# Gates computed inside the prompt pipeline, and one running order of 36 weight tiles over two stages

## The reference, cut to what matters

```python
proj = jnp.einsum('btd,dc->btc', h, w_in)
(a_u, a_g, b_q, b_k, b_v, b_i, b_f, b_o, b_g,
 c_q, c_k, c_v, c_g, d_q, d_g) = jnp.split(proj, SPLIT_POINTS, axis=-1)
...
i_pre = (b_i + gate_bias[0]).astype(jnp.float32)
logf = jax.nn.log_sigmoid((b_f + gate_bias[1]).astype(jnp.float32))
hb, C, n, m = mlstm(b_q.reshape(B, T, ML_HEADS, ML_DK), b_k.reshape(B, T, ML_HEADS, ML_DK),
                    b_v.reshape(B, T, ML_HEADS, ML_DV), i_pre, logf, C0, n0, m0)
...
yc = stick_breaking(c_q.reshape(B, T, SB_HEADS, SB_DIM), k_all, v_all, pos0, sb_bias)
yc = yc.reshape(B, T, GROUP_WIDTH) * jax.nn.silu(c_g)
yd = mem_attention(d_q.reshape(B, T, MEM_HEADS, MEM_DIM), mem_k, mem_v).reshape(B, T, GROUP_WIDTH)
yd = yd * jax.nn.silu(d_g)
```

## Time and profile before

| | us |
|---|---|
| median of 3 runs | 1418.17 |
| lowest, highest | 1414.91, 1420.5 |
| the profiled execution's own time | 1413.02 |
| its span | 1411.3 |
| PE busy | 1247.4 (88%) |
| DVE busy | 807.8 (57%) |
| ACT busy | 471.1 (33%) |
| POOL busy | 373.2 (26%) |

### The profile page before, as it was taken

How to read it: one execution, slowest core, us unless ns; L and a number is a source line. 1 busy time by engine, 2 the same in 40 slices (tenths; PEclk the granted TensorE clock), 3 DMA queues, 4 the chain that set the end, 5 groups by cost and what they waited for, 6 DMA issues and landing times. The chain is left out here.

```text
span 1411.3 us, 22662 instructions
## 1 busy us (share of the span) xinstructions
PE 1247.4 (88%) x7624; PEld 1050.7 (74%) x7624; DVE 807.8 (57%) x1098; ACT 471.1 (33%) x872; POOL 373.2 (26%) x245
## 2 busy tenths in 40 slices
PE   6986999998989637999898994999999999799998
PEld 5884767777766337899898984887878777467886
DVE  5658898998854514868486692344424443524121
ACT  6523556465365412132221314322213131412111
POOL 2475444353400005646556461000000000000000
PEclk9997999999999968999898997999989999899999
DMA  8765576674742408545556531855656544544320
GB/s 292 215 205 192 185 254 192 201 245 145 248 149 87 146 18 253 175 150 181 166 177 206 168 102 56 257 165 154 193 163 205 164 150 149 194 141 146 103 60 30
DMA packets 200917, 235.80 MB, mean 167 GB/s; under 512 B 13555, under 2 KB 122418, under 8 KB 200794
## 3 DMA queue, kind: packets, MB, share of 16 engines
q1 hardware_dynamic: 195682, 218.30, 49.8%
q0 software_dynamic: 5120, 16.06, 3.2%
HBM read 213.78 MB, written 20.63 MB: 166 GB/s over the span
## 5 line engine op out<-in xcount | busy, mean ns | idle before, releaser
L2091 POOL TENSOR_TENSOR bp_keys<-bp_keys,bp_q 128x1024 f32<-128x1024 f32 x64 | 167.0, 2637 | 130.9 <-DMA bp_keys<-cache_sb_k 130.7
L2091 POOL TENSOR_TENSOR cp_keys<-cp_keys,cp_q 128x1024 f32<-128x1024 f32 x64 | 161.8, 2549 | 137.9 <-DMA cp_keys<-cache_sb_k 137.7
L150 PE MATMUL bank<-xh,b_w_hi 128*128 128x344 f32 x480 | 162.3, 338 | 7.0 <-DVE b_w_lo L133 7.0
L150 PE MATMUL bank<-xl,b_w_hi 128*128 128x344 f32 x480 | 157.2, 328 | 0.0
L150 PE MATMUL bank<-xh,b_w_lo 128*128 128x344 f32 x480 | 157.0, 327 | 0.0
L150 PE MATMUL bank<-xh,d_w_hi 128*128 128x344 f32 x384 | 130.6, 340 | 26.9 <-ACT d_w_hi L128 19.3
L246 PE MATMUL bank<-xh,c_w_hi 128*128 128x344 f32 x384 | 129.7, 338 | 0.9 <-DVE c_w_lo L225 0.9
L246 PE MATMUL bank<-xl,c_w_hi 128*128 128x344 f32 x384 | 125.9, 328 | 0.0
L246 PE MATMUL bank<-xh,c_w_lo 128*128 128x344 f32 x384 | 125.8, 328 | 0.0
L150 PE MATMUL bank<-xl,d_w_hi 128*128 128x344 f32 x384 | 125.6, 327 | 0.0
L150 PE MATMUL bank<-xh,d_w_lo 128*128 128x344 f32 x384 | 125.6, 327 | 0.0
(11 more groups left out here) (386 smaller groups left out, 2495.3 us busy)
## 6 DMA issues: line engine op xcount, KB each, us to landing
cp_keys<-cache_sb_k SPq DMA_DIRECT2D x128, 256.0 KB, 2.8
cp_values<-cache_sb_v SPq DMA_DIRECT2D x128, 256.0 KB, 3.0
bp_keys<-cache_sb_k SPq DMA_DIRECT2D x128, 256.0 KB, 3.2
dp_values<-cache_sb_v SPq DMA_DIRECT2D x128, 256.0 KB, 2.8
b_w_raw<-w_in SPq DMA_DIRECT2D x20, 512.0 KB, 5.5
d_w_raw<-w_in SPq DMA_DIRECT2D x16, 512.0 KB
o_raw<-w_out SPq DMA_DIRECT2D x8, 1024.0 KB, 5.4
c_w_raw<-w_in SPq DMA_DIRECT2D x14, 512.0 KB, 5.2
```

What stands on the lines that cost most here:

```text
L150: last = self.nc.tensor.matmul(self.bank(j, c)[:, 0:self.width], w[:, s, k, :], x[:, k, c * self.width:(c + 1) * self.width], start=(k == ...
L2091: self.nc.gpsimd.tensor_tensor(self.keys[:, s], self.keys[:, s], q, ALU.mult).then_inc(self.scaled.sem, 1)
```

## The change

**One flow of tiles.** `Projection` is replaced by `Flow`, made once. It counts 36 tiles in one running order: 20 of the mLSTM and 16 of the memory stage. Tile j lies in slot j % 2; raw tiles lie in the first half of a ring (the buffer in which the prompt's page keys lie until iteration 2), and high and low parts in buffers that the prompt's tiles use too. Its semaphores are never cleared between these stages.

```diff
+    def load(self, sp, j, columns):
+        if j >= 2:
+            sp.wait_ge(self.hi_ready, j - 1)
+            sp.wait_ge(self.lo_ready, j - 1)
+        sp.sem_inc(self.loading, 1)
+        sp.dma_start(self.raw[:, j % 2], columns).then_inc(self.landed[j % 2], 16)
+    def split_hi(self, act, j):
+        act.wait_ge(self.landed[j % 2], 16 * (j // 2 + 1))
+        if j >= 2:
+            act.wait_ge(self.projected, 3 * (j - 1))
+        self.nc.scalar.activation(self.hi[:, j % 2], self.raw[:, j % 2], ACT.Copy).then_inc(self.hi_ready, 1)
```

```diff
+        self.tiles += [("IF", 0), ("G", GT - 1)]
         self.tile_of = {t: j for j, t in enumerate(self.tiles)}
...
-        for n, t in enumerate((("K", i + 1), ("G", i), ("Q", i + 1), ("V", i + 1))):
+        for n, t in enumerate((("K", i + 1) if i + 1 < GT else ("IF", 0), ("G", i), ("Q", i + 1), ("V", i + 1))):
...
                 load_values(i + 1, 0, 4)
+                if i + 2 == GT:
+                    sp.wait_ge(keys.z_ready.sem, keys.z_ready.at(GT - 1, NP))
+                    flow.load(sp, 0, k.w_in[:, :, B_K:B_K + P])
+                    flow.load(sp, 1, k.w_in[:, :, B_V:B_V + P])
...
+                if i == GT - 1:
+                    if u in (SPLIT, SPLIT + 1):
+                        act.wait_ge(stream.projected, stream.made(len(tiles)))
+                        flow.split_hi(act, u - SPLIT)
+                    if u == SOFTEN:
+                        load_tables(nc, act, LN_EXP)
+                        gates.soften(act)
+                        load_tables(nc, act, SIGMOID)
+            load_tables(nc, act, LN_EXP)
+            gates.exponents(act)
...
+                if i == GT - 1:
+                    if u == 3:
+                        stream.wait_taken(dve, tile_of["IF", 0], 2)
+                        gates.add_bias(dve)
+                    if u == SUMS:
+                        gates.sums(dve)
+                    if u == CARRY:
+                        gates.carry(dve)
+                    if u == TOPS:
+                        gates.tops(dve)
+                    if u in (SPLIT, SPLIT + 1):
+                        flow.split_lo(dve, u - SPLIT)
...
                         store(i, 0)
                     if i + 1 < GT:
                         keys.multiply_keys(pool, i + 1, r)
+            pool.wait_ge(keys.z_ready.sem, keys.z_ready.at(GT - 1, NP))
+            gates.load(pool)
+            gates.to_rows(pool)
+            gates.turn_ends(pool)
+            store(GT - 1, 0)
+            gates.turn_carried(pool)
+            gates.store(pool)
             store(GT - 1, 1)
-            pool.wait_ge(mix_out[0], 16 * GT)
-            pool.wait_ge(mix_out[1], 16 * GT)
+            gates.finish(pool)
```

The steps of `Gates` that stand in units 3 to 11:

```diff
+    def to_rows(self, pool):
+        k, G = self.k, self.G
+        pool.wait_ge(self.biased, 1)
+        pool.sem_inc(self.sending, 1)
+        pool.dma_start(k.gates_dram, self.source[0:G, 0:T]).then_inc(self.to_dram, 16)
+        pool.dma_start(k.new_gates_dram, self.source[0:G, T:NT]).then_inc(self.to_dram, 16)
+        pool.wait_ge(self.to_dram, 32)
+        pool.dma_start(self.i_row, k.gates_dram[0:MLH, :].rearrange("h (c t) -> (h c) t", t=P)).then_inc(self.from_dram, 16)
+        pool.dma_start(self.f_row, k.gates_dram[MLH:G, :].rearrange("h (c t) -> (h c) t", t=P)).then_inc(self.from_dram, 16)
+        pool.dma_start(self.new, k.new_gates_dram.rearrange("g b -> b g"),
+                       allow_slow_non_contiguous=True).then_inc(self.from_dram, 16)
+    def soften(self, act):
+        act.wait_ge(self.from_dram, 48)
+        for dst, src, s in ((self.soft, self.f_row, self.row_act), (self.new_soft, self.new[:, MLH:self.G], self.new_act)):
+            self.nc.scalar.activation(dst, src, ACT.Abs).then_inc(s, 1)
+            act.wait_ge(s, 1)
+            self.nc.scalar.activation(dst, dst, ACT.Exp, scale=-1.0).then_inc(s, 1)
+            act.wait_ge(s, 2)
+            self.nc.scalar.activation(dst, dst, ACT.Ln, bias=1.0).then_inc(s, 1)
...
+        dve.wait_ge(self.row_act, 3)
...
+    def turn_ends(self, pool):
+        k = self.k
+        pool.wait_ge(self.row_step, 5)
+        pool.sem_inc(self.sending, 1)
+        pool.dma_start(k.ends_dram.rearrange("k r -> r k"), self.ends, allow_slow_non_contiguous=True).then_inc(self.ends_out, 16)
+        pool.wait_ge(self.ends_out, 16)
+        pool.dma_start(self.end_rows, k.ends_dram.rearrange("(o k) r -> o (k r)", o=1)).then_inc(self.ends_in, 16)
...
+    def carry(self, dve):
+        nc, s, R = self.nc, self.row_step, self.R
+        nc.vector.memset(self.m_row, 0.0).then_inc(s, 1)
+        nc.vector.tensor_tensor_scan(self.soft, self.k.a_rows, self.k.a_rows, FAR * 1e4, ALU.max, ALU.max).then_inc(s, 1)
+        dve.wait_ge(s, 7)
+        dve.wait_ge(self.ends_in, 16)
...
+    def turn_carried(self, pool):
+        k = self.k
+        pool.wait_ge(self.row_step, 12)
+        pool.sem_inc(self.sending, 1)
+        pool.dma_start(k.m_prev_dram.rearrange("(o r) -> o r", o=1), self.m_prev_row).then_inc(self.m_out, 16)
+        pool.wait_ge(self.m_out, 16)
+        pool.dma_start(self.m_prev, k.m_prev_dram.rearrange("(r o) -> r o", o=1),
+                       allow_slow_non_contiguous=True).then_inc(self.m_in, 16)
...
+    def tops(self, dve):
+        nc, s = self.nc, self.row_step
+        dve.wait_ge(self.m_in, 16)
+        nc.vector.tensor_scalar(self.top, self.soft, self.m_prev, None, ALU.max).then_inc(s, 1)
+        dve.wait_ge(s, 13)
```

```diff
+            for half in range(2):
+                sp.wait_ge(k.mix_out[half], 16 * GT)
+            sp.wait_ge(k.mix_done, 16 * MLH)
...
-                    act.wait_ge(mix_out.sem, mix_out.at(i, 0))
+                    act.wait_ge(mix_out, 16 * i)
+                else:
+                    for half in range(2):
+                        act.wait_ge(k.mix_out[half], 16 * GT)
...
-            pool.wait_ge(mix_out.sem, mix_out.at(MLH, 0))
```

**In the mLSTM stage** three sets of rows are transposed at the start (before: one), the last five page keys are loaded ahead of the rows of the next head, and their reductions stand elsewhere on DVE:

```diff
                 load_tile(i + 1, K_)
+                load_keys(i, 13, paged.PAIRS)
                 load_rows(i + 1)
-                load_keys(i, 13, paged.PAIRS)
                 load_tile(i + 1, V_)
...
                 nc.vector.tensor_tensor(C_old[:], C_old[:], wide, ALU.mult).then_inc(carried.sem, 1)
-                reduce_keys(i, 11, 14)
...
                 last.then_inc(C_new_ready.sem, 1)
-                reduce_keys(i, 14, paged.PAIRS)
-                paged.add_bias(dve, i)
+                reduce_keys(i, 11, 13)
...
                 nc.vector.tensor_tensor(h[:, T:NT], h[:, T:NT], sig[:, T:NT], ALU.mult).then_inc(h_ready.sem, 1)
+                reduce_keys(i, 13, paged.PAIRS)
+                paged.add_bias(dve, i)
```

**In the memory stage** tiles 0 and 1 of head i+1 are split in head i:

```diff
+                take(2, u[:, PAD:PAD + NT], ACT.Copy)
+                if i + 1 < MLH:
+                    flow.split_hi(act, tile(i + 1, 0))
                 act.wait_ge(a_free.sem, a_free.at(i, 0))
-                proj.take(act, i, 3, lambda c: mix_a[:, c * CH:(c + 1) * CH], ACT.Silu)
+                take(3, mix_a, ACT.Silu)
+                if i + 1 < MLH:
+                    flow.split_hi(act, tile(i + 1, 1))
...
+                if i + 1 < MLH:
+                    flow.split_lo(dve, tile(i + 1, 0))
                 gated(1)
+                if i + 1 < MLH:
+                    flow.split_lo(dve, tile(i + 1, 1))
```

More of the change, by code:

```diff
@@ L1331, in pages, with multiply @@
                     paged.weigh(pe, i, 2 * WEIGHED_BEFORE[j, c])
+            def multiply(i, j):
+                flow.multiply(pe, tile(i, j), {c: lambda c=c: pages(i, j, c) for c in range(3)})
             for i in range(MLH):
@@ L2031, with __init__ @@
     PAIRS = NPG // 2
-    def __init__(self, ctx, nc, k, tag, first, count, ring, sums, weights):
+    def __init__(self, ctx, nc, k, tag, first, count, ring, sums, weights, keys=None):
         sb = lambda name, shape, dt=F32: ctx.enter_context(nc.sbuf_tensor(f"{tag}_{name}", shape, dt))
```

505 lines of the change are left out of this document (216 added, 289 removed).

## The result

The changed kernel takes 1359.34 us (median of 4 runs, 1357.2 to 1365.6); the kernel before, on the same chip, 1419.34 us (median of 4). The ratio is 0.9598, with a 95% interval of 0.9569 to 0.9627. The forecast was 1357 us, with a range of 1338 to 1377. The profiled execution has a span of 1355.5 us against 1411.3, so 55.8 us less; the sum had said 59.0, and by the medians it is 60.0. PE is busy for 1228.2 us of the span, against 1247.4: of the 55.8 us, 36.6 are idle time of PE and 19.2 are busy time.

The account below looks back on a forecast made before the run. PE, busy 88% of the span, was taken as the bound, with time to regain where it idles or does less. Four terms sum to 59.0 us: 1413.0 to 1354.0, forecast 1357 on the median's scale, range 1338 to 1377.

Parts of the forecast that it names:

- B: mLSTM stage: without three reductions ahead, DVE reaches the new matrices earlier and PE's wait for them goes; 13.8 us gained.
- D: Starts of the memory heads: splits placed in the head before end PE's waits of 7.7 us, plus clock; 10 us gained.
- A: First junction, prompt to mLSTM: 49.1 us of gates' stretch replaced by work in iteration 3 and a shorter end; 30.3 gained.
- C: Second junction, ahead of the memory stage: PE's wait falls from 19.3 to 14.4 us, for the bank's memset; 4.9 gained.
- The gates' tile: Units 0 to 2 of iteration 3: 11.4 us of PE, less 3.34 idle and 2.8 by the clock; cost 5.
- The other steps of the gates: ACT and DVE work added to iteration 3, mostly covered by idle time in units 6 to 9; cost 2 us.
- The trip through DRAM: Iteration 3: two hops, 6.2 us, fit into two units of 7 to 10, the second pair barely; cost 1.5 us.
- R1: Iteration 3: DVE is held by the trips through DRAM, 6 us per pair of hops; 1369 us, chance 0.10.
- Head 0: First mLSTM head: rows copied and page keys, started later, can hold it up; cost 1.3 us (0 to 3).
- R2: mLSTM stage: the wait turns into one for page keys, giving 4 us instead of 13.8; 1367 us, chance 0.08.
- R3: Both junctions: tiles not split in time or the barrier with its DMAs costs as before; 1380 us, chance 0.05.
- R4: DVE in units 9 and 11: slower than before, each hop exposed by 16.5 us beyond its cover; 1425 us, chance 0.02.

Follow-up runs that it names:

- the seven kernels: Kernels with the gates' steps in the units where the change has them; iteration 3 takes 87.7 to 89.7 us in them, 88.6 in the mean.
- the three with the old prompt: Kernels whose prompt stage is as before the change, without any step of the gates in iteration 3; 52.7 us behind unit 3.
- first experiment: Changed kernel with DVE's old order in the mLSTM stage (three key reductions ahead of the new matrices), SP's order kept new: 1359.18 us, ratio 0.9599.
- third: Kernel before with only SP's order changed, the last three pairs of page keys loaded ahead of the next head's rows: 1398.33 us, ratio 0.9865.

## Why the prediction was right, point by point

The time was within 3 us of the forecast, and the sum within 3.2 of what the traces show. The places were the right ones. But the terms are off in both directions, and in B and D the size came out for another reason than the one given; that the sum fits so well is in part luck.

| term | predicted | measured |
|---|---|---|
| A, first junction with iteration 3 and head 0 | 30.3 | 22.5 |
| B, mLSTM stage | 13.8 | 17.2 |
| C, second junction | 4.9 | 3.8 |
| D, memory heads | 10 | 10.9 |
| output stage | 0 | 1.4 |
| sum | 59.0 | 55.8 |

**A.** The end of the stage was taken as 9 and is 9.6. *Iteration 3* was to grow by 5 + 2 + 1.5 = 8.5 and grew by 9.9 (89.7 against 79.8; the seven kernels have 88.6 in the mean, and the three with the old prompt 79.2, which is 9.4). *The gates' tile*, priced at 5, was right, in size and in mechanism. Up to unit 3 the iteration has grown by 5.3 us (31.57 against 26.24), and the three parts of the working are there: PE's idle time fell by 3.0, the clock rose from 0.87 to 1.00, and busy PE grew by 8.3, which is 11.4 less 3.1 by the clock. Before (busy PE stands behind the length):

```profile
406.76:433.00 26.24, 20.10 (x147) 15.94 (x144) 13.60 (x26) 16.70 (x35) 0.58 (x1) 0.87 0.21 71
```

*The other steps of the gates* were priced at 2 and cost nothing that can be seen: without the ends' trip, the part behind unit 3 is as short as in the kernels with the old prompt. *The trip through DRAM* was costed as two hops of 3.1 us from the earlier trace rows, 6.2 together, and "both fit". The trip from 472.16 to 484.84 takes 12.7 us: the store lands after 7.7 us and the read back after 4.6, with the pages' loads beside them (the DMA engines are 0.96 busy from 472.2 to 479.9). In the eight kernels in which DVE waits for it, the trip takes 12.0 to 13.9 us.

```profile
ends<-ring POOLq DMA_DIRECT2D x1, 0.2 KB, 7.7
ring<-ends POOLq DMA_DIRECT2D x1, 0.2 KB, 4.6
```

That is R1's mechanism, which had a chance of 0.10 and a price of 12: it did occur, for the first pair of hops alone, at 4.3 us by the kernel without the trip, where the forecast had 1.5 for both pairs. The 2 that were too much and the 2.8 that were too little nearly cancel. *Head 0* of the mLSTM was to give back 1.3 and gave back 5.1 (27.6 to 22.5). The page keys start later against the tiles than before, and DVE, in order, comes late to the weighted keys, for which PE waits 3.9 us. *The start*: 2.1 us were lost before iteration 3, within what kernels with one and the same code show.

**B.** The wait of 13.8 us is gone, as predicted, but of the step "without the three reductions DVE comes to the new matrices earlier" only the smaller part was the cause: with the keys in time the work of the three costs PE 1.9 us of waits (first experiment) or 4.2 (third), and the rest of the 13.8 was the wait of the third one. Two edits of the change cure it, and the prediction counted on one. That R2 didn't come to pass fits this: with the new order of DVE alone, too, no wait moved to the halves of h. And the 17.2 us are not 13.8 and 3.4 more. From the scores of head 0 to the h of head 3 (length, busy PE; the clock is the third number from the end), before and after:

```profile
576.79:851.59 274.80, 260.64 (x1613) 251.59 (x1612) 200.26 (x291) 67.52 (x109) 149.79 (x72) 0.94 0.53 165
```

```profile
554.29:811.90 257.61, 248.04 (x1612) 238.32 (x1611) 217.24 (x291) 68.69 (x110) 153.22 (x72) 0.99 0.57 180
```

PE's idle time fell by only 4.6 us, since 9.5 us of other waits came, 8.0 of them for the carried matrices, which the prediction had not costed. The same matmuls took 12.6 us less, by the clock, which the text had only in its upper bound, with 1.7. The 9.5 us one way and the 12.6 the other were both left out, and nearly cancel. Before, PE ran at 0.57 of its clock behind the longest of the waits (679.0 to 690.4); after, the same operations (start and duration; before, then after):

```profile
681.03 3.41 PE L2018 MATMUL bank<-b_qT,b_C_new 128*128 128x1 f32 x16
...
690.45 1.03 PE L1971 MATMUL bank<-ident,b_v_diag 128*128 128x128 f32 x8
```

```profile
652.63 1.84 PE L2053 MATMUL bank<-b_qT,b_C_new 128*128 128x1 f32 x16
658.45 1.03 PE L2006 MATMUL bank<-ident,b_v_diag 128*128 128x128 f32 x8
```

From one to the other it is 9.4 us before and 5.8 after, and there are four such places. One sign didn't come: DVE doesn't wait for PE any more ahead of the halves of h (4.88 us in the earlier trace rows), so the cover there is used up.

**C.** As predicted, PE waits for the clearing of the bank, 15.5 us where 14.4 were worked out. The store of mix was assumed to give 2.6 and gives 1.1, as the run with the stores waited for shows.

**D.** No wait at the head starts, as predicted, and 10.9 us less. But here too the parts differ: 3.9 us of new waits for pages of values, which the prediction had not costed, stand against 6.4 us less of busy PE, where 2.3 were allowed for the clock. First before, then after:

```profile
883.34:1211.26 327.92, 309.25 (x1832) 253.48 (x1833) 134.73 (x293) 80.11 (x156) 8.48 (x16) 0.93 0.57 175
```

```profile
839.85:1156.85 317.00, 302.88 (x1832) 247.90 (x1833) 133.64 (x292) 80.05 (x156) 8.82 (x16) 0.96 0.58 182
```

Putting the splits back costs 13.8, half of it by the clock.

**R3 and R4** have nothing in their favour: both tiles are ready at both junctions, and the dearest hop lands 5.1 us later than the 2.6 it was priced with, not 16.5.

**The table loads.** The Trainium skill's page "ScalarE: Activation LUTs", section "What ACT_TABLE_LOAD costs", would have added 4.1 us of drains. In the changed kernel a load at 461.67 of 1.28 us is followed by an operation at 462.97, so here too no pause behind it is seen, and none ahead of it, where ACT's last operation ends at 461.65:

```profile
461.67 1.28 ACT L87 ACT_TABLE_LOAD   x1
462.97 0.31 ACT L202 ACTIVATE ring<-ring 32x128 f32<-32x128 f32 x1
```

## What to carry to other kernels

When an engine waits, split what stands ahead of it into its work and its own wait: here three reductions cost PE 1.9 us of waits once their data was there, and an edit on the loading queue was worth as much as the one on the computing engine. Before you credit a change with an effect, undo each part alone and both together; of two redundant cures each looks worthless. A step that is moved beside a heavy load stream should be priced with DMAs that ran beside such a stream, not with the fastest row of its size. And a wait of PE that goes away can give more than its length, since the clock rises too, while the next wait may take a part of the room: in the mLSTM stage these two, 12.6 and 9.5 us, were both left out of the sum. An experiment that makes a step cheaper and gains nothing shows that another limit lies close below, not that the step was free.

## What the runs showed of the hardware that was not expected

A store of 0.2 KB, element by element, from POOL landed after 7.7 us beside loads of 256 KB pages, where one of 0.5 KB had 2.6 us in the kernel before; the two differ in both, and no run separates the elements from the loads. Taking 63 matmuls, some 10 us of PE, out of a pipeline changed its length by half a microsecond, since PE then idled 5.4 us more and ran at 0.60 of its clock for ten. And kernels with the same prompt code reached the same operation between 406.8 and 416.5 us, with PE's waits for pages of values in iteration 3 between 3.4 and 7.6 us: a difference of a few microseconds between single runs of this kernel says nothing by itself.
